# First modulation loads in 4 KB rows and in halves, small loads on another queue, first lower part on one engine

## What is computed

```
mod = silu(c) @ w_ada + b_ada                       # 1 x 6144: shift1, scale1, gate1, shift2, scale2, gate2
h   = rms_norm(x) * g1 * (1 + scale1) + shift1
z   = h @ W_in + b_in                               # 5376 columns: u, v, q, k, values, two gates
ya  = gelu(u) * (w_spatial * mask @ layer_norm(gelu(v)) + b_spatial)
yb  = windowed attention with sinks and partial rotary
x   = x + gate1 * ((sigmoid(gA) * (ya @ w_oA) + sigmoid(gB) * (yb @ w_oB)) @ w_out)
h2  = rms_norm(x) * g2 * (1 + scale2) + shift2
x   = x + gate2 * MoE(h2)                           # top 4 of 32 experts, clamped SwiGLU, width 1024
out = rms_norm(x) * g_final
```

## Time and profile before

| | us |
|---|---|
| median of 3 runs | 1353.52 (1350.73 to 1355.14) |
| the profiled execution | 1354.68 |
| its span | 1352.9 |
| PE busy | 1079.2 (80%) |
| DVE busy | 417.3 (31%) |
| ACT busy | 225.1 (17%) |
| POOL busy | 97.9 (7%) |
| DMA | 473.22 MB, mean 350 GB/s |

### The profile page before, as it was taken

How to read it: one execution, slowest core, us unless ns; L and a number is a source line. 1 busy time by engine, 2 the same in 40 slices (tenths; PEclk the granted TensorE clock), 3 DMA queues, 4 the chain that set the end, 5 groups by cost and what they waited for, 6 DMA issues and landing times.

```text
span 1352.9 us, 25998 instructions
## 1 busy us (share of the span) xinstructions
PE 1079.2 (80%) x10218; PEld 498.8 (37%) x10219; DVE 417.3 (31%) x988; ACT 225.1 (17%) x433; POOL 97.9 (7%) x43
## 2 busy tenths in 40 slices
PE   3689999987986688666999799997666797866964
PEld 1457677873431122112443344343111133311422
DVE  1487687974221111111222222222111122211214
ACT  2112123033111001000121112121000011100102
POOL 0154344100000000000000000000000000000001
PEclk9699999995997878878999999999887798978977
DMA  9786964687999999999789989649999987999990
GB/s 308 253 321 234 350 233 170 203 343 280 417 417 418 417 417 417 417 415 416 289 362 415 416 342 417 286 189 417 416 418 416 416 338 307 417 415 416 416 403 35
DMA packets 113388, 473.22 MB, mean 350 GB/s; under 512 B 12832, under 2 KB 16672, under 8 KB 80416
## 3 DMA queue, kind: packets, MB, share of 16 engines
q1 hardware_dynamic: 110880, 469.03, 86.9%
q10 hardware_dynamic: 2432, 3.02, 0.8%
HBM read 470.98 MB, written 1.05 MB: 349 GB/s over the span
## 4 chain that ended last, share of the span: by engine, by line
PE 35%; SPq 30%; DMA 25%; issue 4%; DVE 3%; ACT 2%; POOL 0%; ACTq 0%; DVEq 0%
SPq L359 14%; SPq L353 13%; PE bank L1600 12%; PE bank L1257 11%; DMA gate_up<-in_w_down_dram 10%; PE bank L1636 5%; DMA down<-in_w_down_dram 5%; DMA gate_up<-in_w_gate_up_dram 5%; DMA down<-in_w_gate_up_dram 2%; DMA gate_up<-in_w_ada_dram 2%; PE bank L1567 1%; PE bank L1553 1%; DMA gate_up<-in_w_in_dram 1%; PE bank L1279 1%; SPq L348 1%
## 5 line engine op out<-in xcount | busy, mean ns | idle before, releaser
L1600 PE MATMUL bank<-gate_up,mod 128*32 128x512 f32 x2592 | 359.7, 679 | 121.2 <-DMA gate_up<-in_w_gate_up_dram 75.2
L1187 DVE TENSOR_SCALAR front<-bank 128x256 f32<-128x256 f32 x50 | 21.2, 425 | 708.7 <-PE bank L1600 708.7
L1600 PEld LDWEIGHTS bank<-gate_up,mod 128*32 128x32 f32 x2592 | 78.5, 117 | 334.8 <-DMA gate_up<-in_w_gate_up_dram 168.6
L1636 PE MATMUL bank<-gate_up,mod 128*32 128x256 f32 x2496 | 152.1, 387 | 39.4 <-DMA gate_up<-in_w_down_dram 35.7
L1257 PE MATMUL bank<-gate_up_r 128*128 128x512 f32 (+1 forms) x544 | 137.0, 397 | 16.7 <-DVE gate_up_r L749 11.1
L1257 PEld LDWEIGHTS bank<-gate_up_r 128*128 128x128 f32 x544 | 100.3, 192 | 45.4 <-issue 22.3
L1636 PEld LDWEIGHTS bank<-gate_up,mod 128*32 128x32 f32 x2496 | 74.6, 110 | 105.8 <-DMA gate_up<-in_w_down_dram 52.1
L1600 PE MATMUL bank<-down,mod 128*32 128x512 f32 x608 | 87.9, 693 | 31.4 <-DMA down<-in_w_gate_up_dram 29.3
L720 ACT ACTIVATE front<-front 128x256 f32<-128x256 f32 x50 | 20.8, 417 | 537.6 <-DVE front L1187 537.6
L328 POOL TENSOR_TENSOR gate_up_r<-gate_up,gate_up_r 128x2048 fp32r<-128x2048 f32 (+1 forms) x14 | 88.7, 6339 | 117.6 <-DVE gate_up_r L749 117.6
L527 POOL TENSOR_TENSOR gate_up<-x_sb,gate_up 128x1024 f32<-128x1024 f32 x2 | 4.7, 2348 | 1031.6 <-DVE x_sb L1210 1031.6
(11 more groups left out here) (256 smaller groups left out, 815.8 us busy)
## 6 DMA issues: line engine op xcount, KB each, us to landing
gate_up<-in_w_gate_up_dram SPq DMA_DIRECT2D x204, 1024.0 KB, 20.8
gate_up<-in_w_down_dram SPq DMA_DIRECT2D x104, 1024.0 KB, 23.0
down<-in_w_gate_up_dram SPq DMA_DIRECT2D x52, 1024.0 KB, 20.8
gate_up<-in_w_ada_dram SPq DMA_DIRECT2D x12, 2048.0 KB, 9.5
down<-in_w_down_dram SPq DMA_DIRECT2D x24, 1024.0 KB, 24.6
gate_up<-in_w_in_dram SPq DMA_DIRECT2D x10, 2048.0 KB, 14.5
gate_up<-in_w_o_a_dram SPq DMA_DIRECT2D x2, 2048.0 KB, 7.8
gate_up<-in_w_o_b_dram SPq DMA_DIRECT2D x2, 2048.0 KB, 10.3
```

Source lines behind the costliest of these rows:

```text
L1187: dve.tensor_scalar(g_cap, banks[4][:, 0:HW], LIMIT, None, ALU.min).then_inc(ev("g_ready"), 1)
L1600: last = pe.matmul(banks[4][q * BM:(q + 1) * BM, :], xT[:, k % KG, k // KG, :], w[:, :, q * HW:(q + 1) * HW], start=(k == 0), stop=(k == K ...
L1636: last = pe.matmul(banks[7][q * BM:(q + 1) * BM, 0:HW], hidT[:, k % KG, k // KG, :], w[:, k % 2, q * HW:(q + 1) * HW], start=(k == 0), sto ...
```

## The change

- The modulation's first four parts come as two pairs (1024 columns, so rows of 4 KB), each pair in two loads that split the summed dimension: chunks 0 to 3, then 4 to 7. TensorE adds the first half of both parts of a pair when its load is in, then the second. Pair 0 lies in what are ring rooms 0 and 1, pair 1 in the room of the two upper parts. The wait for `cond_in` on SP's queue is gone, and the pair loads are issued right behind x. Ring room 3 is free for ada4 from the start, ring room 2 for u0.
- The thirteen small loads are issued by GpSimd, behind the last `rows_made`, ahead of the mask of w_spatial. SP goes from v0 to ada4, v0's bias, v1, its bias and u0.
- ScalarE scales both tiles. VectorE casts v0's weights in that time, and makes the whole lower part of v0's weights itself, between the parts of tile 0 and those of tile 1; GpSimd's halves begin with v1.

```diff
--- before.py
+++ after.py
@@ -80,11 +80,10 @@
     def ring_slot(name):
 
         if name.startswith("ada"):
-            j = int(name[3:])
-            s, nth = (j - 1, 1) if 1 <= j <= RING else (RING, max(1, j - 2))
+            s, nth = RING, int(name[3:]) - 3
         else:
             i = names.index(name)
-            s, nth = i % RING, i // RING + 2
+            s, nth = i % RING, i // RING + 1
         return s, 16 * nth
 
 
@@ -133,6 +132,7 @@
 
         def columns(buf):
             return buf.rearrange("p a (b n) -> p (a b) n", n=COLS)
+        pair = [gate_up[1 - i][:, 0:4, :].rearrange("p a (b n) -> p (a b) n", n=2 * COLS) for i in range(2)]
         ring = [columns(gate_up[1][:, 2 * i:2 * i + 2, :]) for i in range(RING)] + [columns(gate_up[0][:, 6:8, :])]
 
         w_upper = [columns(gate_up_r[0][:, 2 * i:2 * i + 2, :]) for i in range(2)]
@@ -266,6 +266,7 @@
         x_in, cond_in, gmlp_in, attn_in, route_in = (sem(n) for n in ("x_in", "cond_in", "gmlp_in", "attn_in", "route_in"))
         c_in, b_ada_in, ln_in, g2_in, gf_in, bd_in, stored = (sem(n) for n in ("c_in", "b_ada_in", "ln_in", "g2_in", "gf_in", "bd_in", "stored"))
         exp_bias_in = sem("exp_bias_in")
+        pair_in = [sem(f"pair_in{i}") for i in range(4)]
         ring_in = [sem(f"ring_in{i}") for i in range(RING + 1)]
         bias_in = [sem(f"bias_in{i}") for i in range(2)]
         z_full = [sem(f"z_full{i}") for i in range(NZ)]
@@ -320,7 +321,7 @@
         def t_done(ins, name):
             ins.then_inc(t_free[t_use(name)[0]], 1)
 
-        shared = [i for i in range(len(dense)) if i < names.index("ob1")]
+        shared = [i for i in range(len(dense)) if 0 < i < names.index("ob1")]
 
         def lower(eng, i, chunks):
 
@@ -379,7 +380,12 @@
         def _(sp):
             sp.dma_start(c_col, c[0].rearrange("(k p) -> p k", p=P)).then_inc(c_in, 16)
             sp.dma_start(x_sb[:, :, :], x[0].rearrange("(t p) d -> p t d", p=P)).then_inc(x_in, 16)
-            sp.wait_ge(cond_in, 80)
+            for i in range(2):
+                for a in range(2):
+                    chunks = slice(4 * a, 4 * a + 4)
+                    sp.dma_start(pair[i][:, chunks, :],
+                                 w_ada[0, :, 2 * i * COLS:(2 * i + 2) * COLS].rearrange("(k p) n -> p k n", p=P)[:, chunks, :])\
+                      .then_inc(pair_in[2 * i + a], 16)
 
             def load(name, w, used=None):
                 if used:
@@ -398,26 +404,12 @@
                     cols = dense[i][2].shape[1]
                     sp.dma_start(bias_ring[:, i % 2, 0:cols],
                                  dense[i][2].to_broadcast([P, cols])).then_inc(bias_in[i % 2], 16)
-            for j in range(4):
-                load_ada(j)
             load(*dense[0][:2], "ada1")
+            load_ada(4)
             load_bias(0)
-
-            sp.dma_start(ws, w_spatial[0].rearrange("h i j -> i h j")).then_inc(gmlp_in, 16)
-            sp.dma_start(bs, b_spatial[0].rearrange("h i -> i h")).then_inc(gmlp_in, 16)
-            sp.dma_start(pos_i[:, :], positions[0].rearrange("(t p) -> p t", p=P)).then_inc(attn_in, 16)
-            for hh in range(2):
-                for r in range(2):
-                    sp.dma_start(sk[hh * CH:(hh + 1) * CH, r, :],
-                                  sinks[0:1, :].rearrange("a (g m) -> a m g", m=4)[:, 2 * hh + r, :].to_broadcast([CH, 4]))\
-                       .then_inc(attn_in, 16)
-            sp.dma_start(wr, w_router[0].rearrange("(k p) e -> p k e", p=P)).then_inc(route_in, 16)
-            sp.dma_start(br, b_router[0:1, :].to_broadcast([P, E])).then_inc(route_in, 16)
-            load_b_ada(sp, 4, 12, b_ada_in)
-            load_ada(4, "ada0")
-            load(*dense[1][:2], "ada2")
+            load(*dense[1][:2], "ada1")
             load_bias(1)
-            load(*dense[2][:2], "ada3")
+            load(*dense[2][:2])
             for i in range(len(dense) - RING):
                 if 5 + i < 12:
                     load_ada(5 + i, f"ada{4 + i}")
@@ -498,6 +490,19 @@
             pool.affine_select(out=row_sel, in_=row_sel, compare_op=ALU.not_equal, fill=1.0, base=0,
                                pattern=[[-QR, NQT], [0, P]], channel_multiplier=1).then_inc(ev("consts"), 1)
 
+            pool.wait_ge(ev("rows_made"), 4)
+            pool.dma_start(ws, w_spatial[0].rearrange("h i j -> i h j")).then_inc(gmlp_in, 16)
+            pool.dma_start(bs, b_spatial[0].rearrange("h i -> i h")).then_inc(gmlp_in, 16)
+            load_b_ada(pool, 4, 12, b_ada_in)
+            pool.dma_start(pos_i[:, :], positions[0].rearrange("(t p) -> p t", p=P)).then_inc(attn_in, 16)
+            for hh in range(2):
+                for r in range(2):
+                    pool.dma_start(sk[hh * CH:(hh + 1) * CH, r, :],
+                                   sinks[0:1, :].rearrange("a (g m) -> a m g", m=4)[:, 2 * hh + r, :].to_broadcast([CH, 4]))\
+                        .then_inc(attn_in, 16)
+            pool.dma_start(wr, w_router[0].rearrange("(k p) e -> p k e", p=P)).then_inc(route_in, 16)
+            pool.dma_start(br, b_router[0:1, :].to_broadcast([P, E])).then_inc(route_in, 16)
+
             pool.wait_ge(gmlp_in, 32)
             pool.memset(ws[0:CH, :, CH:P], 0.0).then_inc(ev("ws_masked"), 1)
 
@@ -564,14 +569,15 @@
                 part_copy(j)
 
             act.wait_ge(ev("mod_col_ready"), 2)
-            for h in range(2):
-                name = f"xT1{h}"
-                bank = z_wait(act, name)
-                for i in range(4):
-                    k = 4 * h + i
-                    last = act.activation(hT[:, k, P:2 * P], bank[:, i * P:(i + 1) * P], ACT.Identity,
-                                          bias=mod_col[:, 0, k:k + 1], scale=mul1[:, k:k + 1])
-                z_done(last, name)
+            for t in range(TILES):
+                for h in range(2):
+                    name = f"xT{t}{h}"
+                    bank = z_wait(act, name)
+                    for i in range(4):
+                        k = 4 * h + i
+                        last = act.activation(hT[:, k, t * P:(t + 1) * P], bank[:, i * P:(i + 1) * P], ACT.Identity,
+                                              bias=mod_col[:, 0, k:k + 1], scale=mul1[:, k:k + 1])
+                    z_done(last, name)
 
             for t in range(TILES):
                 z_wait(act, f"xT{t}1")
@@ -822,22 +828,13 @@
                                  banks[5][:, :].rearrange("p (m n) -> p m n", n=QR)[:, :, 0]))
             dve.scalar_tensor_tensor(mul1, mod_col[:, 1, :], 1.0, g1_col, ALU.add, ALU.mult)\
                .then_inc(ev("mod_col_ready"), 2)
-            dve.wait_ge(ev("mod_col_ready"), 2)
-            for h in range(2):
-                name = f"xT0{h}"
-                bank = z_wait(dve, name)
-                for i in range(4):
-                    k = 4 * h + i
-                    last = dve.tensor_scalar(hT[:, k, 0:P], bank[:, i * P:(i + 1) * P], mul1[:, k:k + 1],
-                                             mod_col[:, 0, k:k + 1], ALU.mult, ALU.add)
-                z_done(last, name)
+            w_parts_upper(0)
             for t in range(TILES):
                 for h in range(2):
                     z_gone(dve, f"xT{t}{h}")
                 x_parts(hT, upper_a, hT_lower, "hT_parts", slice(t * P, (t + 1) * P))
                 if t == 0:
-                    w_parts_upper(0)
-            w_parts_lower(0)
+                    w_parts_lower(0)
             w_parts_upper(1)
             w_parts_lower(1)
 
@@ -1313,9 +1310,20 @@
 
             pe.wait_ge(ev("crep_ready"), 1)
             pe.wait_ge(ev("heads_ready"), 1)
-            for j in range(4):
-                ada(j)
-                ada_rows(j, banks[6][:, j * P:(j + 1) * P]).then_inc(ev("rows_made"), 1)
+            for i in range(2):
+                if i:
+                    pe.wait_ge(ev("part_out"), 2)
+                for a in range(2):
+                    pe.wait_ge(pair_in[2 * i + a], 16)
+                    for j in range(2):
+                        for q in range(NQT):
+                            last = pe.matmul(banks[4 + j][q * QR:(q + 1) * QR, :], crep[:, 4 * a + q, :],
+                                             pair[i][:, 4 * a + q, j * COLS:(j + 1) * COLS], start=(a == 0), stop=(a == 1),
+                                             skip_group_check=True)
+                        if a:
+                            last.then_inc(ev("ada_made"), 1)
+                for j in (2 * i, 2 * i + 1):
+                    ada_rows(j, banks[6][:, j * P:(j + 1) * P]).then_inc(ev("rows_made"), 1)
             pe.wait_ge(ev("ada_added"), 1)
             for j in range(4):
                 last = pe.transpose(banks[5][:, j * P:(j + 1) * P], mod[:, j, :], ident[:, :])
```

## The result

The change made the kernel slower by 0.23%: 1355.47 us (median of 15 runs) against 1352.67 (15 runs), a ratio of 1.0023 with a 95% interval of [1.0014, 1.0032]. The forecast was 1341.0 with a range of 1336 to 1353, so it was wrong, and in sign too. The profiled execution took 1353.47 us with a span of 1350.9; by medians the span grew from 1350.9 to 1352.9 and what lies outside it from 1.8 to 2.5.

What follows compares the result with a forecast made beforehand. Weight loads pace the experts and TensorE bounds attention once fed, so the loose start counts: v1t0's third pass gains 12.5 us after small loads and v1's landing overlap. 1353.52 - 12.5 = 1341.0 us; range 1336 to 1353.

Steps and rivals of the forecast that it cites:

- Step 1: Modulation start: no cond_in wait and 4 KB rows bring the last half's matmuls to near 28.6, gain 4.2 us.
- Step 2: ScalarE scales alone, VectorE casts v0: v0t0 starts near 41, 6.3 us earlier, and v0t1 ends near 54.
- Step 3: Thirteen small loads on GpSimd take 24.4 us, ending near 58; third pass of v1t0 starts at 65.2, 12.7 earlier.
- Rival (b): GpSimd's issuing stands while VectorE casts, perhaps subtracts; list grows 6.0 to 12.9 us, gain 3.3, 1350.2; chance 0.18.
- Rival (c): Each small piece costs GpSimd 8.6 ns, list 47.5 us; third pass of v1t0 10.4 later, 1363.9; chance 0.12.
- rival (a): Everything hidden: GpSimd emits quickly, v1 lands by 52; third pass of v1t0 at 61.5, gain 16.4, 1337.1; chance 0.22.
- Step 4: Small transfers share DMA engines with v1, which lands from 45.6 to 60.6; its cast starts at 51 to 57.
- same formula as in the forecast: From v1's landing to the third pass of v1t0: landing at 60.6 starts it at 69.6, 8.3 us earlier.
- What it gains, the kernel gains: Whatever the start of v1t0's third pass (before 77.92) gains arrives whole at the kernel's end; 12.5 us taken.
- a gain taken back by the clock or by waits for DMA after 70 us: Stated sign of a wrong forecast: clock or DMA waits take the gain back after 70; no size given.
- the third pass: TensorE's third pass of v1t0, the forecast's clock event: from 77.92 to near 65, 12.5 us earlier taken.

Runs made afterwards that it cites:

- e5: Changed kernel with all thirteen small loads issued by ScalarE, behind its ln_v loads, instead of GpSimd; time not given in the text, v1's cast starts at 51.90.
- e6: Changed kernel with GpSimd issuing only the five loads of 512-byte rows (w_spatial, b_ada), ScalarE the eight others; 1346.5 us, 0.41% won.
- e2: Changed kernel with the thirteen small loads back on SyncE, everything else of the change kept; gains 0.32% against the kernel before.
- e17: Changed kernel plus 52 already-met waits (26 instructions) in SyncE's program ahead of its experts' loop; ratio 0.9976 to the kernel before.
- e4: The changed kernel, unaltered, measured once more beside the other runs; ratio 1.0018 to the kernel before.
- e18: e6 plus the same 26 waiting instructions in SyncE's program ahead of the experts' loop; 1341.86 us, 0.73% below the kernel before.
- e3: Kernel before with only the thirteen small loads moved from SyncE to GpSimd; 1359.03 us, costs 0.42%.
- e1: Kernel before with one load, the positions (1 KB), issued by GpSimd instead of SyncE; costs nothing that its interval shows.
- e9: Changed kernel plus a second copy of the thirteen small loads on SyncE near 118 us, into free room; time not given in the text.
- e10: e6 plus a second copy of the thirteen small loads on SyncE near 118 us, into free room; time not given in the text.
- e12: Kernel before, its list kept, plus a second copy of the thirteen small loads on SyncE near 118 us; time not given in the text.
- e16: e6 with v1 issued ahead of ada4 and the eight ScalarE small loads moved to SyncE behind u0; time not given in the text.

## Why the prediction was wrong

- **Step 1 right, with some luck.** The stream runs at 408 GB/s (taken 417); the last half's matmuls start at 29.49 (forecast near 28.6), 0.9 late. From there to ScalarE's first scaling I kept 7.54 us; it took 6.45, the last sixteen matmuls 2.57 instead of 3.64. So the rows are made at 33.42 (33.6) and the scaling starts at 35.94 (36.15) because two errors of about 1 us cancel.
- **Step 2 right.** v0's cast 36.26 (36.2), v0t0 41.11 (41.1), v0t1 ended near 53.7 (54.4), ada4 53.69 (54.4 by the forecast), ws transposes over at 56.6 (57.4). The rates that I took for v0t0 make 5.7 us of its first sixteen matmuls, not the 6.2 that they were read from; it comes to half a us.
- **Step 3 wrong in size, to no harm.** The list took GpSimd 10.8 us, not 24.4. Rival (b) is not borne out: v0's cast and the parts ran beside those issues (36.26 to 41.06). The "DVE blocks DMA" box of the Trainium skill ("SBUF — State Buffer") would have had them stand still; their issue times here show no such thing, while the writing of the descriptors itself is not visible in the trace. Rival (c), 47.5 us, is refuted too; rival (a) fell with step 4.
- **Step 4 failed.** "v1 lands from 45.6 to 60.6. At 56 its cast ends 58.3": the cast began at 63.59. I priced the small transfers by the engine time that they took on SyncE's queue, at most 15 us, where they stand in one line with the weights. On queues of their own they and ln_v take turns with the weights packet by packet (275 of q1 beside 272 and 278 from 42 to 50 us), so q1 moved 1.06 MB from 38 to 50 us where e5 moved 3.24, and 8 to 30 GB/s from 50 to 54. With the same formula as in the forecast (60.6 gives 8.3) a landing at 63.3 gives 5.6; 5.1 was measured. e6, where the elements are gone from that queue, measured 12.2.
- **"What it gains, the kernel gains" failed.** The 5 us at the first expert were lost again. They come back when SyncE's program ahead of the loop gets its thirteen loads again (e2) or 26 waits in their place (e17), so it was the place of the loop in the program that cost them and not the transfers, if the waits move nothing else that counts. The forecast looked for a gain taken back by the clock or by waits for DMA after 70 us; that a loop of untouched code would start elsewhere in its engine's program was in none of my cases. By e17 it is 0.4 to 0.5% (0.9976 against 1.0023 and, in e4, 1.0018), more than the whole loss; by e18 against e6 0.3%.
- **The account of the miss.** From 12.5 earlier to 2.8 later are 15.3 us: 7.4 at the third pass, 0.2 from there to the first sigmoid, 6.9 in the experts' part by medians, 0.7 outside the span.
- **Outside the span** I assumed no change; it grew by 0.7. Without the list it is 2.0 (e2, e5), with the rows alone on GpSimd 2.0 to 2.1, in e3 1.8. So neither part makes it alone; this stays open.

With both repaired (e18) the kernel takes 1341.86, where 1341.0 was forecast for a mechanism that fitted the start only. That the two are so near is partly luck: e18 is 10.3 us below its own before (1352.19), and the forecast was for 12.5.

Open: why the fetches fall where they do and which positions between 78 and 82, or above 97, are good; how they delay the landing of loads; that the packets of q14 are SyncE's is inferred from their going with SyncE's program and its gaps. e1, e9, e10 and e12 have stages shorter than before by 1.6 to 3.2, which the position doesn't explain (before's profiled execution was itself 2.0 above its median); nearly all of that comes after the fifteenth sigmoid. e3's and e16's +6 against +1.4 to +3.7 elsewhere isn't settled either.

## What to carry to other kernels

A load that seems cheap to issue can starve a stream on another queue. Count what each queue gets in packets, and look at GB/s beside the DMA share in windows of 2 to 4 us. Of what was tried on the second queue, rows of 512 bytes held the stream up least (v1 cast 4.6 us later than with nothing there), single elements more (8.4), both together most (11.7); sending them when no stream is awaited wasn't tried. When instructions leave or join an engine's program ahead of a long loop, compare the packets of the instruction queues before and after and the engine's gaps in the loop; padding by a few met waits is a cheap test. Carry a gain seen at one event to the end by reading the shift at several later events rather than one.

## What the runs showed of the hardware

- 4 KB rows of w_ada alone came at 408 GB/s (window from 14 us), 2 KB rows at 387.
- GpSimd's queue packs 8 rows of 512 bytes into a packet, and 24 smaller pieces on the average (5,504 in 400, and 16 more packets a load); SyncE's has a packet a piece. A packet of small pieces held an engine for 0.88 us near 52 us (after), and for 0.015 near 7.5 us (e1).
- Three queues with work at the same time got 272, 275 and 278 packets from 42 to 50 us (after), of 1.7, 1.9 and 3.6 KB on the average.
- A loop of 212 SyncE instructions with its start at 70 to 78 went with 25 more instruction packets in six turns than at 82 to 97, and with stops of 10.4 and 10.5 us between two issues (e6, after) where padding left 1.9 (e18, e17).
